# Sixteen experts' gate and up weights in three places instead of two, loaded in fixed order

## The chip, the cores and the metric

The kernel runs on one core of one Trainium2 chip. The metric is the device time of one launch in microseconds, the median of three runs. The core has five engines: TensorE (PE, with its weight loads PEld), VectorE (DVE), ScalarE (ACT), GpSimd (POOL) and SyncE (SP), which here only issues DMA transfers.

## What is computed

The reference is one layer of a hybrid model over 16 meta tokens and 1024 tokens of width 1024: a norm, one projection, three mixers (S5, HGRN2, differential attention), an output projection, and a mixture of experts, then a final norm. The change touches the experts alone:

```python
    group_prob = jax.nn.softmax((t @ w_group).astype(f32) + b_group.astype(f32), axis=-1)
    gp, gi = lax.top_k(group_prob, 1)
    ...
    ev, ei = lax.top_k(in_group, MOE_TOP_K)
    ew = jax.nn.softmax(ev, axis=-1) * gp
    expert_id = gi * MOE_EXPERTS_PER_GROUP + ei
    ...
    for e in range(MOE_EXPERTS):
        he = jax.nn.silu(t @ w_gate[e]) * (t @ w_up[e])
        y = y + gates[:, e:e + 1] * (he @ w_down[e])
```

There are 16 experts in four groups, and each token goes to two experts of one group. An expert has gate and up weights of 1024 x 512 each and down weights of 512 x 1024, all float32: 2 MB each, 6 MB an expert. With the reference's inputs the experts get between 59 and 196 of the 2048 rows. In blocks of 128 rows these are 1, 1, 2, 2, 1, 1, 1, 1, 1, 2, 1, 2, 2, 2, 2, 2 blocks, 24 in all, so experts 4 to 8 have one block each, one after another.

## The kernel before

The first half of the program (projection, mixers, attention, output projection) is the same in both kernels. Then VectorE works out the routing (`dve_route`): the slot of each token-expert pair, the number of blocks of each expert, and tables with one entry for each block. SP waits for `tables_ready`, the other engines read the number of block pairs.

The expert stage runs over the blocks. Every engine has its own instruction stream: blocks 0 and 1 are written out, then a loop over pairs of blocks with two bodies in it (`blocks`), then the last pair. The body of block b holds, on TensorE: the turn of the hidden values of b, gate and up of block b + 1 (8 chunks), the turn of the token rows of b + 2 (L2257), and down of block b (4 chunks). A chunk is 128 rows of weights by 1024 columns. Products are made in three passes from split operands: the higher part of a number (rounded to fp32r) and the lower part (the rest), so each chunk has six products (L2277): four with the higher weights, then two with the lower ones.

The higher part of a chunk is cast by ScalarE (L2323), the lower part is a subtraction of the higher part from the raw weights. Chunks 1, 2 and 3 of every four are subtracted by VectorE (L2375), the fourth by GpSimd (L2220). Both parts go through a ring of four chunks (`RING`); a cast waits until TensorE has used the chunk four before it (`chunk_used`). VectorE also makes the hidden values (L2393), the lower part of the rows (L2381), scales the outputs (L2401) and makes the lower part of the hidden values (L2442). GpSimd also gathers the rows of block b + 2 (L2207) and adds outputs into `h_d` (L2247).

Which place of the raw weights a block reads is a number from a table. Each engine reads it into a register at the head of a body: `buffers` (L2193) reads the table `ebuf` for b and for b + 1, two reads (L2191), between the last operation of the body before and the first cast or subtraction of this one.

SP issues the raw weights. Raw gate and up weights have two places, raw down weights two. For each block, SP reads six table entries (L2174), waits for its place, and issues four gate and up transfers (L2180) and one down transfer (L2185). Where the expert is the same as that of the block before, the transfers are issued with a condition that makes them empty. Each waits until the one before it has landed.

Of the kernel before, what the change touches and what calls it, by code (L numbers as in the profile page):

```python
# [13 lines left out]
F32 = mybir.dt.float32  # L14
F32R = mybir.dt.float32r
BF16 = mybir.dt.bfloat16
I32 = mybir.dt.int32
ACT = mybir.ActivationFunctionType
ALU = mybir.AluOpType
AX = mybir.AxisListType  # L20

P = 128
# [28 lines left out]
C_COS = 976  # L51
# [7 lines left out]
MEM = 48432  # L59
# [4 lines left out]
SPLIT = 5 * D + RING * 2 * D  # L64


def constants():
# [22 lines left out]
    c[:, C_IOTAB:C_IOTAB + NB] = np.arange(NB)  # L90
    inv = (np.float32(1.0) / (np.float32(10000.0) ** (np.arange(0, 64, 2, dtype=np.float32) / np.float32(64)))).astype(np.float32)
# [19 lines left out]
def build(nc, a, out):  # L111
    ctx = ExitStack()
    with ctx:
# [11 lines left out]

        with (nc.sbuf_tensor("below_split", [P, NT * D], F32), nc.sbuf_tensor("split", [P, SPLIT], F32R) as split_tensor,
              nc.sbuf_tensor("below_weights", [P, O_C - NT * D - SPLIT], F32),
              nc.sbuf_tensor("weights", [P, 2 * 3 * D * FF // P], F32) as weights_tensor):
            split, weights = split_tensor, weights_tensor
        with (nc.sbuf_tensor("below_x", [P, O_X], F32), nc.sbuf_tensor("xsplit", [P, 2 * KD * L], F32R) as xsplit_tensor,  # L130
# [10 lines left out]
        MLOE_T = split_at("mix_early_lower", MEM - 512, 512)  # L141
        WOL_T = [split_at("wo_lower%d" % k, O_C + 2 * KD * FF + 1024 * k, 1024) for k in range(KD)]
# [1736 lines left out]
        NEW, OLD, RUN, PRV, BUF, NHALF, NPR = take(NB), take(NB), take(NB), take(NB), take(NB), take(1), take(1)  # L1879
        PCMP = take(NB // 2)  # L1880
# [8 lines left out]
        eblk, ebuf, enew = (sml[:, o:o + NB].bitcast(I32) for o in (506, 570, 398))  # L1889
        efree2 = sml[:, 104:104 + NB].bitcast(I32)  # L1890
        efree, edown, npair = sml[:, 366:366 + NB].bitcast(I32), sml[:, 334:334 + NB].bitcast(I32), sml[:, 504:505].bitcast(I32)
# [36 lines left out]
        def dve_route(dve, link):  # L1928
# [39 lines left out]
            link(ts(BLK[:, 0:2], BLK[:, 0:2], 1.0, None, ALU.max))  # L1968
# [42 lines left out]
            link(nc.vector.tensor_copy(eblk[:, :], EBF))  # L2011

            scan = nc.vector.tensor_tensor_scan
            link(nc.vector.memset(NEW[:, 0:1], 1.0))
            link(tt(NEW[:, 1:NB], EBF[:, 1:NB], EBF[:, 0:NB - 1], ALU.not_equal))
            link(ts(OLD, NEW, -1.0, 1.0, ALU.mult, ALU.add))
            link(tt(PRV, NEW, con[:, C_IOTAB:C_IOTAB + NB], ALU.mult))
            link(scan(RUN, OLD, PRV, 0.0, ALU.mult, ALU.add))
            link(nc.vector.memset(PRV[:, 0:1], 0.0))
            link(tt(PRV[:, 1:NB], NEW[:, 1:NB], RUN[:, 0:NB - 1], ALU.mult))  # L2020
            link(scan(BUF, OLD, PRV, 0.0, ALU.mult, ALU.add))
            link(ts(PRV, BUF, 12.0, 1.0, ALU.mult, ALU.add))
            link(ts(RUN, PRV, 9.0, None, ALU.min))
            link(stt(RUN, PRV, -8.0, RUN, ALU.add, ALU.max))
            link(nc.vector.tensor_copy(efree, RUN))
            link(ts(RUN, RUN, 4.0, None, ALU.add))
            link(nc.vector.tensor_copy(efree2, RUN))
            link(ts(BUF, BUF, 0.0, 12.0, ALU.is_gt, ALU.mult))
            link(tt(PRV, PRV, BUF, ALU.add))
            link(nc.vector.tensor_copy(edown, PRV))  # L2030
            link(tt(OLD, OLD, NEW, ALU.subtract))
            link(scan(BUF, OLD, NEW, 1.0, ALU.mult, ALU.add))
            link(nc.vector.tensor_copy(ebuf, BUF))
            dve_rows_lower(dve, 0, 0)
            link(stt(NEW, EBF, 1.5, NEW, ALU.is_gt, ALU.mult))
            link(nc.vector.tensor_copy(enew, NEW))
            link(ts(NHALF, CB[:, NE - 1:NE], 0.5, None, ALU.mult))
            link(tt(PCMP, NHALF.to_broadcast([P, NB // 2]), con[:, C_IOTAB:C_IOTAB + NB // 2], ALU.is_gt))
            link(red(NPR, PCMP, AX.X, ALU.add))
            link(ts(NPR, NPR, float(-(LEAST // 2)), None, ALU.add))  # L2040
            nc.vector.tensor_copy(npair, NPR).then_inc(tables_ready, 1)

        def dve_slot_hot(dve, link):
# [8 lines left out]
            link(nc.vector.tensor_copy(HOTW[:, :, 0], HOT))  # L2052
            for i in range(3):
# [22 lines left out]
        WGU = weights[:, 0:4 * KD * FF].rearrange("p (k i n) -> p k i n", i=2, n=FF)  # L2076
        WDN = weights[:, 4 * KD * FF:].rearrange("p (k n) -> p k n", n=D)
        oS = NT * D
# [7 lines left out]
        WH, WL = ([take_split(D) for _ in range(RING)] for _ in range(2))  # L2086
# [24 lines left out]
        def raw(kind, k, q):  # L2111
# [3 lines left out]
            if kind == "gu":  # L2115
                return WGU[:, bass.ds(q * KD + k, 1)].rearrange("p a i n -> p (a i n)")
# [38 lines left out]
        def sp_experts(sp):  # L2155
# [10 lines left out]
            sp.dma_start(WDN[:, 0:FF // P], a["w_down"][0].rearrange("(k p) n -> p k n", p=P)).then_inc(first_loaded, 16)  # L2166
            sp.wait_ge(xg_loaded[0], 16)
            sp.dma_start(WDN[:, FF // P:2 * FF // P], a["w_down"][1].rearrange("(k p) n -> p k n", p=P)).then_inc(wdn_loaded, 16)
            sp.wait_ge(first_loaded, 48)
            sp.wait_ge(tables_ready, 1)  # L2170

# [451 lines left out]
```

## Time and profile before

| | |
|---|---|
| median of 3 runs | 1196.14 us (1190.55 to 1201.69) |
| span of the profiled execution | 1192.0 us (its own time is shown as this span) |
| granted TensorE clock, mean | 0.966 |
| PE busy | 1065.8 us (89%) |
| DVE busy | 843.0 us (71%) |
| ACT busy | 638.6 us (54%) |
| POOL busy | 487.2 us (41%) |
| DMA, mean | 164 GB/s |
| L2277, expert products | 1728, 418.1 us busy |
| L2375, lower parts on DVE | 216, 300.9 us busy |
| L2220, lower parts on POOL | 72, 205.0 us busy |

The span is the time from the first to the last instruction of one execution. Busy time is the union of an engine's operations; the ends of matmuls are modelled. The expert stage begins at about 700 us and ends at about 1162 us; before it stand 58% of the span, which the change does not touch apart from the routing tables.

### The profile page before, as it was taken

To read this page: it belongs to the slowest core of one execution; us is meant where nothing else is said; L and a number is where in the kernel's file an instruction comes from. 1 tells how busy PE (TensorE), PEld (TensorE's weight loads), DVE (VectorE), ACT (ScalarE), POOL (GpSimd) and SP (SyncE) were. 2 spreads that over 40 slices of the span, in tenths; PEclk is the share of its full clock that TensorE was granted. 3 is DMA by queue.
4 is the path that set the end of the run, shared out by engine and by line. 5 is a ranking of instruction groups with operands and counts; after the bars stand their busy time and mean duration, and the time that the engine had idled before them with its cause. 6 is when DMAs were issued, how large, how long until landed. Compare 5 with 4: busy or idle time off the path is not lost. (4 is left out here: it accounts for less than half of the span.)

```text
span 1192.0 us, 22049 instructions
## 1 busy us (share of the span) xinstructions
PE 1065.8 (89%) x7126; PEld 888.2 (75%) x7126; DVE 843.0 (71%) x1234; ACT 638.6 (54%) x1008; POOL 487.2 (41%) x303
## 2 busy tenths in 40 slices
PE   4899998999969989999999648999999999999995
PEld 4898998889968646666667536878777887888873
DVE  5797857563357556555554497888887999899987
ACT  5522111166533456444443326778776887888854
POOL 1121211122000226111111114878775887999960
PEclk9999999999988989999999859999999999999988
DMA  7216434332033820011111774788999878877454
GB/s 266 80 48 73 118 95 127 102 114 71 21 72 80 319 71 1 19 54 53 54 66 59 280 267 159 238 257 305 322 379 371 275 266 286 258 266 229 103 160 161
DMA packets 89495, 194.97 MB, mean 164 GB/s; under 512 B 9265, under 2 KB 32049, under 8 KB 88769
## 3 DMA queue, kind: packets, MB, share of 16 engines
q1 hardware_dynamic: 82800, 169.91, 42.0%
q0 software_dynamic: 6624, 24.12, 8.5%
q8 instruction: 45, 0.74, 0.3%
q14 instruction: 26, 0.20, 0.1%
HBM read 220.60 MB, written 31.51 MB: 211 GB/s over the span
## 5 line engine op out<-in xcount | busy, mean ns | idle before, releaser
L2277 PE MATMUL ps<-split 128*128 128x512 f32 x1728 | 418.1, 398 | 15.8 <-DVE split L2375 8.1
L2277 PEld LDWEIGHTS ps<-split 128*128 128x128 f32 x1728 | 322.4, 190 | 93.3 <-DVE split L2375 12.8
L2323 ACT CAST split<-weights 128x1024 fp32r (+1 forms) x288 | 298.2, 1052 | 101.9 <-PE ps L2277 80.4
L2375 DVE TENSOR_TENSOR split<-weights,split 128x1024 fp32r<-128x1024 f32 x216 | 300.9, 1446 | 46.5 <-ACT split L2323 45.0
L480 PE MATMUL ps<-xsplit,wsplit 128*128 128x384 f32 (+2 forms) x1440 | 239.7, 324 | 4.0 <-POOL wsplit L252 4.0
L2220 POOL TENSOR_TENSOR split<-weights,split 128x1024 fp32r<-128x1024 f32 x72 | 205.0, 2847 | 91.4 <-ACT split L2323 90.4
L480 PEld LDWEIGHTS ps<-xsplit,wsplit 128*128 128x128 f32 x1440 | 226.2, 189 | 5.4 <-POOL wsplit L252 4.6
L252 POOL TENSOR_TENSOR wsplit<-mem,wsplit 128x1024 fp32r<-128x1024 f32 x22 | 57.1, 2597 | 247.7 <-ACT wsplit L335 247.7
L1605 DVE TENSOR_REDUCE sml<-ps 128x1 f32<-128x1040 f32 (+7 forms) x64 | 46.6, 769 | 61.6 <-PE ps L1785 61.6
L1722 ACT COPY mem<-ps 128x512 f32<-128x512 f32 (+3 forms) x48 | 21.4, 481 | 109.3 <-PE ps L1804 71.7
L1548 POOL TENSOR_TENSOR sml<-sml 128x4 f32<-128x4 f32 x8 | 8.1, 1015 | 156.2 <-DVE sml L1626 156.2
L335 ACT CAST wsplit<-mem 128x1024 fp32r<-128x1024 f32 x22 | 23.2, 1053 | 85.1 <-DMA mem<-in_w_in 85.1
L2247 POOL DMA_INDIRECT h_d<-par,sml x22 | 53.0, 2408 | 3.4 <-issue 3.0
L1661 ACT ACTIVATE mem<-ps,sml 128x1040 f32<-128x1040 f32 (+7 forms) x64 | 47.1, 736 | 0.0
L1810 PE MATMUL ps<-mem 128*128 128x128 f32 x288 | 39.3, 282 | 7.1 <-ACT mem L1722 7.1
L2207 POOL DMA_INDIRECT con<-xn_d,sml x24 | 37.7, 1571 | 19.3 <-POOL sml L2204 19.3
L1810 PEld LDWEIGHTS ps<-mem 128*128 128x128 f32 x288 | 34.7, 191 | 12.6 <-ACT mem L1722 12.2
L1785 PE MATMUL ps<-mem 64*128 64x400 f32 (+6 forms) x224 | 42.4, 493 | 0.0
L419 ACT COPY mem<-ps 128x384 f32<-128x384 f32 (+2 forms) x48 | 20.3, 451 | 40.9 <-PE ps L480 34.6
L2328 ACT CAST split<-ps 128x512 fp32r<-128x512 f32 x48 | 25.7, 589 | 17.8 <-PE ps L2257 17.8
L1026 POOL TENSOR_TENSOR sml<-sml 128x16 f32<-128x16 f32 x2 | 7.6, 3800 | 66.6 <-DVE sml L1231 66.6
L2401 DVE TENSOR_SCALAR par<-ps,sml 128x512 f32<-128x512 f32 x44 | 30.9, 744 | 5.1 <-DMA h_d<-par,sml 5.1
(434 smaller groups left out, 1631.1 us busy)
## 6 DMA issues: line engine op xcount, KB each, us to landing
weights<-in_w_down SPq DMA_DIRECT2D x26, 2048.0 KB, 15.9
weights<-in_w_gate SPq DMA_DIRECT2D x50, 1024.0 KB
weights<-in_w_up SPq DMA_DIRECT2D x50, 1024.0 KB
mem<-in_w_in SPq DMA_DIRECT2D x22, 512.0 KB, 4.4
mem<-in_x SPq DMA_DIRECT2D x10, 512.0 KB, 3.5
mem<-in_w_out SPq DMA_DIRECT2D x1, 4096.0 KB, 14.8
h_d<-mem SPq DMA_DIRECT2D x8, 512.0 KB, 2.6
xn_d<-mem SPq DMA_DIRECT2D x8, 512.0 KB, 2.6
```

What stands on the lines that cost most here:

```text
L252: nc.gpsimd.tensor_tensor(WLO[i], RAW[i], WHI[i].bitcast(F32), ALU.subtract).then_inc(wlo_ready, 1)
L480: mm = nc.tensor.matmul(ps[:, n % 6, 0:hi - lo], w[slot_of(h)][:, k % 4, P * m:P * m + P], x[:, k, lo:hi], start=(k == 0 and p_ == 0), sto ...
L1605: nc.vector.tensor_reduce(NMX[:, 2 * (n % 2) + c:2 * (n % 2) + c + 1], logits(c)[:, KEY0:KEY0 + keys_of(n)], AX.X, ALU.max, negate=True).t ...
L1661: f(PR_[n % 2][:, c, 0:nk], logits(c)[:, KEY0:KEY0 + nk], ACT.Exp, bias=NMX[:, o:o + 1], accum_out=SUM[:, o:o + 1]).then_inc(exp_done, 1)
L1785: mm = nc.tensor.matmul(logits(c)[:, s:e], AQ[R, h, P * i:P * i + P], AK[R, h, s - lo:e - lo], start=(e != hi), stop=True, skip_group_chec ...
L1810: nc.tensor.matmul(b[:, 0:P], AT[n % 2][:, k], V[:, 1 + k, vc], start=(k == 0), stop=False)
L2207: pool.indirect_dma_start(XG[:, par], None, xn_d, bass.IndirectOffsetOnAxis(ap=ixc[:, par:par + 1], axis=0)).then_inc(xg_loaded[par], 16)
L2220: nc.gpsimd.tensor_tensor(WL[place % RING], raw(kind, k, q), WH[place % RING].bitcast(F32), ALU.subtract).then_inc(wl_pool, 1)
L2247: pool.indirect_dma_start(h1_d, bass.IndirectOffsetOnAxis(ap=sixc[:, 1 - par:2 - par], axis=0), YE, None, compute_op=ALU.add).then_inc(ye_ ...
L2277: mm = nc.tensor.matmul(ps[:, bank + h, :], x, w[place % RING][:, 512 * h:512 * h + 512], start=(k == 0 and p_ == 0), stop=(k == n - 1 and ...
L2323: nc.scalar.copy(WH[place % RING], raw(kind, k, q)).then_inc(wh_ready, 1)
L2375: nc.vector.tensor_tensor(WL[place % RING], raw(kind, k, q), WH[place % RING].bitcast(F32), ALU.subtract).then_inc(wl_dve, 1)
```

## The change

The gate and up weights get a third place, at the start of the memory, where the routing tables are worked out before. Expert e lies in place e mod 3 for gate and up and e mod 2 for down. These two numbers stand in a constant table (`C_GUB`, `C_DNB`) indexed by the expert. The load tables on VectorE go (`ebuf`, `enew`, `efree`, `efree2`, `edown`); one table of the expert of each block (`etab`) and one of when an expert's gate and up are used up (`half_free`) are left. SP's loop over blocks becomes a written-out list over experts: gate and up of e + 1, then down of e. An engine now finds its place by reading the expert of the block, and then the place of that expert. The lower part of the first rows moves from the middle of the tables to the slot weights. An empty expert would get one block; with these inputs there is none.

```diff
-MEM = 48432
+MEM = 48416
...
+UNIT = 128
+GU_AT = (O_C, O_C + 2 * KD * FF, 0)
...
+    c[:, C_GUB:C_GUB + NE] = np.array([GU_AT[e % 3] // UNIT for e in range(NE)], np.int32).view(np.float32)
+    c[:, C_DNB:C_DNB + NE] = np.array([e % 2 for e in range(NE)], np.int32).view(np.float32)
...
-            link(ts(BLK[:, 0:2], BLK[:, 0:2], 1.0, None, ALU.max))
+            link(ts(BLK, BLK, 1.0, None, ALU.max))
...
-            link(nc.vector.tensor_copy(eblk[:, :], EBF))
-
-            scan = nc.vector.tensor_tensor_scan
-            link(nc.vector.memset(NEW[:, 0:1], 1.0))
...
-            nc.vector.tensor_copy(npair, NPR).then_inc(tables_ready, 1)
+            link(nc.vector.tensor_copy(npair, NPR))
+            link(ts(CB, CB, 12.0, float(gu_used(-1) - KD // 2), ALU.mult, ALU.add))
+            nc.vector.tensor_copy(half_free, CB).then_inc(tables_ready, 1)
...
-                for half in range(2):
-                    sp.wait_ge(w_loads[half], 32 * b + 32)
-                    sp.wait_ge(chunk_used, (free, free_second)[half])
...
+            sp.wait_ge(slots_ready, 2)
+            sp_gate_up(sp, 2, None)
+            free = sp_half_free(sp, 0)
+            for e in range(2, NE):
+                if e + 1 < NE:
+                    free_next = sp_half_free(sp, e - 1)
+                    sp_gate_up(sp, e + 1, free)
+                sp_down(sp, e, free)
+                free = free_next
...
+        def expert_of(eng, b):
+            return eng.value_load(etab[0:1, bass.ds(b, 1)], min_val=0, max_val=NE - 1)
 
         def buffers(eng, b, par, last):
 
-            q = buffer_of(eng, b)
-            return q, (buffer_of(eng, b + 1) if has(par, last, 1) else None)
+            e = expert_of(eng, b)
+            q = eng.value_load(dn_at[0:1, bass.ds(e, 1)], min_val=0, max_val=1)
+            if not has(par, last, 1):
+                return q, None, e, None
+            e_next = expert_of(eng, b + 1)
+            return q, eng.value_load(gu_at[0:1, bass.ds(e_next, 1)], min_val=0, max_val=max(GU_AT) // UNIT), e, e_next
...
-                        act.wait_ge(w_loads[k // 4], 32 * b + 96)
+                        act.wait_ge(w_loads[k // 4], 32 * e_next + 32)
```

VectorE, the end of the loop and the head of what follows it, before. `L2381` is the lower part of the rows, `TENSOR_LOAD` a read of a table into a register, the last row the first subtraction of a block:

```order
L2381 TENSOR_TENSOR split<-ps,split 128x512 [waits xh_ready]
L2144 ISA
L2144 COMPARE_AND_BRANCH
L2191 ISA
L2191 TENSOR_LOAD sml
L2191 ISA x3
L2191 TENSOR_LOAD sml
L2191 ISA x2
L2374 ISA
L2375 ISA [waits wh_ready]
L2375 TENSOR_TENSOR split<-weights,split 128x1024
```

The same place in the changed kernel:

```order
L2393 TENSOR_TENSOR split<-ps,split 128x512 [waits xh_ready]
L2131 ISA
L2131 COMPARE_AND_BRANCH
L2199 TENSOR_LOAD sml
L2199 ISA x2
L2204 TENSOR_LOAD con
L2204 ISA x2
L2208 TENSOR_LOAD con
L2208 ISA x2
L2386 ISA
L2387 ISA [waits wh_ready]
L2387 TENSOR_TENSOR weights_lower<-gate_up,weights_higher 128x1024
```

Rows that only repeat are left out: the read of L2199 stands there twice, ahead of L2204 and ahead of L2208, so two reads have become four, each with its own register instructions, and the read of L2204 or L2208 needs the result of the one ahead of it.

SP, one expert of the written-out list in the changed kernel. L2175 reads `half_free`, L2188 is gate and up, L2196 is down:

```order
L2175 TENSOR_LOAD sml
L2175 ISA x2
L2188 DMA gate_up<-in_w_gate 128x4x512 [waits chunk_used,first_half_loaded]
L2188 DMA gate_up<-in_w_up 128x4x512
L2184 REGISTER_ALU [waits chunk_used,second_half_loaded]
L2188 DMA gate_up<-in_w_gate 128x4x512 [waits chunk_used]
L2188 DMA gate_up<-in_w_up 128x4x512
L2194 REGISTER_ALU [waits wdn_loaded]
L2196 DMA weights<-in_w_down 128x4x1024 [waits chunk_used]
```

Before, each block had six such reads (L2174) ahead of the same five transfers; now each expert has one, and there is no loop.

## Rows read from the trace of the kernel before

**Rows 1.** Waits from 690 us on: waiter, releaser, total us, times, longest.
```profile
ACT split L2323 <- DMA weights<-in_w_up: 16.3, 5, 3.8
PE ps L2257 <- DMA con<-xn_d,sml: 7.2, 1, 7.2
```

**Rows 2.** Chain of waits, row turns (L2257): start us, us, what.
```profile
739.64 0.87 PE ps L2257 x8
848.96 0.87 PE ps L2257 x8
927.69 0.87 PE ps L2257 x8
981.30 0.88 PE ps L2257 x8
1002.43 0.87 PE ps L2257 x8
1020.16 0.87 PE ps L2257 x8
1037.89 0.87 PE ps L2257 x8
1055.64 0.87 PE ps L2257 x8
1127.13 0.87 PE ps L2257 x8
```

**Rows 3.** Stretches: us, busy PE, PEld, DVE, ACT, POOL, PEclk, DMA share, GB/s.
```profile
820.00:838.00 18.00, 18.00 (x88) 14.99 (x87) 14.63 (x16) 14.41 (x17) 13.61 (x9) 1.00 0.67 200
848.80:868.60 19.80, 18.48 (x85) 14.46 (x84) 15.85 (x16) 13.86 (x17) 13.07 (x10) 1.00 1.05 376
1020.00:1037.70 17.70, 17.70 (x85) 14.73 (x84) 15.46 (x15) 14.34 (x17) 15.40 (x10) 1.00 0.79 263
```

**Rows 4.** Register reads, L2191, 1037 to 1046: ns min/median/max, first and last start.
```profile
L2191 DVEq TENSOR_LOAD <-sml x2: 307/794/1281, 1040.7 to 1042.4; - x2
L2191 DVEq SEQ_ASSERT  x2: 23/23/23, 1042.2 to 1042.9; - x2
L2191 ACTq SEQ_ASSERT  x2: 18/18/18, 1039.3 to 1039.9; - x2
```

**Rows 5.** Timelines, ordinary turn from 1037.89: start us, us, what [idle before, releaser].
```profile
1043.22 3.50 DVE L2375 TENSOR_TENSOR split<-weights,split 128x1024 fp32r<-128x1024 f32 x3 [1.14 <-ACT split L2323]
1045.80 3.19 POOL L2220 TENSOR_TENSOR split<-weights,split 128x1024 fp32r<-128x1024 f32 x1 [0.47 <-ACT split L2323]
1044.46 1.05 ACT L2323 CAST split<-weights 128x1024 fp32r x1 [0.31 <-PE ps L2277]
1044.45 11.19 PE L2277 MATMUL ps<-split 128*128 128x512 f32 x48
```

**Rows 6.** Timelines, turn from 1055.64, first half of the loop.
```profile
1061.21 3.50 DVE L2375 TENSOR_TENSOR split<-weights,split 128x1024 fp32r<-128x1024 f32 x3 [1.32 <-ACT split L2323]
1063.54 3.44 POOL L2220 TENSOR_TENSOR split<-weights,split 128x1024 fp32r<-128x1024 f32 x1 [0.22 <-ACT split L2323]
1058.56 2.00 ACT L2323 CAST split<-weights 128x1024 fp32r x2 [0.20 <-issue]
```

**Rows 7.** Timelines, turn from 981.30.
```profile
989.29 3.43 DVE L2375 TENSOR_TENSOR split<-weights,split 128x1024 fp32r<-128x1024 f32 x1
989.20 2.44 POOL L2220 TENSOR_TENSOR split<-weights,split 128x1024 fp32r<-128x1024 f32 x1
992.78 6.06 PE L2277 MATMUL ps<-split 128*128 128x512 f32 x24 [1.00 <-DVE split L2375]
1000.31 2.11 PE L2277 MATMUL ps<-split 128*128 128x512 f32 x8 [1.47 <-DVE split L2375]
```

**Rows 8.** Timelines, turn from 1002.43.
```profile
1006.84 3.50 DVE L2375 TENSOR_TENSOR split<-weights,split 128x1024 fp32r<-128x1024 f32 x3 [0.73 <-ACT split L2323]
1010.33 2.40 POOL L2220 TENSOR_TENSOR split<-weights,split 128x1024 fp32r<-128x1024 f32 x1 [1.38 <-ACT split L2323]
```

## What the change does to the time, predicted blind

> **What bounds the kernel now.** I read the waits first, then the chain of waits, then DMA by stretches, then single engines inside one block of the expert stage. All durations are of one profiled execution with a span of 1192.0 us; the median of the runs, 1196.14, is 4.1 above it, and I add that 4.1 at the end.
>
> The waits [rows 1] name what the change aims at: ScalarE stood 16.3 us, in five waits, for gate and up weights. They also show that the first block begins when its gathered rows land (TensorE waits 7.2 us for that DMA), not when a table is ready.
>
> The chain of waits [rows 2] has one row for each turn of token rows (L2257). From one such row to the next I call a turn; there are 21 of them, 739.64 to 1127.13, together 387.5 us. Three kinds are to be seen. Ordinary turns take 17.73 (1020.16 to 1037.89) and 17.75. The four turns 848.96 to 927.69 take 78.7, or 19.7 each: those are the experts with one block each. The turn from 981.30 takes 21.13, with an expert of two blocks, and it is the one that decides my forecast.
>
> The stretches [rows 3] explain the slow four: DMA runs at 376 GB/s with its share full, against 263 in an ordinary turn. 19.8 us at 376 GB/s are 7.4 MB; in 17.7 us this would take 420 GB/s, more than any stretch shows. Before them, 820 to 838, it runs at 200. So loads that start earlier can remove this loss.
>
> **Inside a turn** TensorE is fed through a ring of four chunks: ScalarE casts, VectorE subtracts for three of four, GpSimd for the fourth. Take t = 0 at the turn's L2257 row. In the turn 1037.89 [rows 5], TensorE starts gate and up at 6.56 (1044.45), and a chunk takes 1.37 (48 products in 11.19, with 0.2 of the last one's tail). The lower parts come in its last two products of six, so it needs subtraction 1, 2, 3 by 7.5, 8.8, 10.2. VectorE starts the first at 5.33 and does three in 3.50, so the third begins at 5.33 + 2.28 = 7.6. GpSimd asks for its own subtraction, the fourth, at 7.91, after ScalarE's cast that starts at 6.57. It is 0.3 us after VectorE's third has begun.
>
> The turn from 981.30 shows what happens in the other order [rows 7]. GpSimd asked at 989.20 (7.90), VectorE's third subtraction came at 989.29 (7.99) and took 3.43 us instead of 1.2: it stood still for nearly the whole of GpSimd's 2.44. TensorE waited 1.0 and later 1.47, when the same thing happened at the second group of chunks. The page SBUF — State Buffer of the Trainium skill (SBUF: two separate sides) says that a VectorE operation with two SBUF inputs and a GpSimd operation share a port pair that the first holds to its end; the trace agrees, 3.43 against 1.2. So a turn costs 17.73 when VectorE comes first and 21.13 when GpSimd does: **3.4 us for being 0.09 us late**.
>
> How near is the edge elsewhere? In the turn 1055.64, the first half of the loop [rows 6], the third begins at 5.57 + 2.28 = 7.85 and GpSimd asks at 7.90: 0.05 us of margin. In the turn right after a collision [rows 8] VectorE is ahead: first subtraction at 4.41, third at 6.69, GpSimd at 7.90, margin 1.2.
>
> **The change, part by part.**
>
> *Third place and fixed order of loads.* It removes SP's six table reads for each block, and it lets gate and up of expert e + 1 go out ahead of down of e. With the reference's inputs every expert has rows, so both kernels load sixteen experts and compute the same 24 blocks: no byte and no product is added. The four turns can fall from 78.7 to 4 x 17.73 = 70.9: gain **7.8 us**, at most 16.3 by the waits. I take 7.8; the rest of the waits was hidden behind the ring.
>
> *Shorter table chain on VectorE before the first block.* About 25 small operations go. The first block starts at the landing of the rows [rows 1], so I count 0; expert 2's load now waits for the second slot table instead, and has a whole block until its use: 0.
>
> *Reads from tables in each block.* VectorE, ScalarE and GpSimd read two numbers into registers for each block now, and four after it. This is the price. On VectorE they stand between the last row subtraction and the first weight subtraction, and VectorE is idle during them. The first read takes 1.28 because it waits for the engine to drain; the second takes 0.31, and the checks behind the two follow each other at 0.7 [rows 4]. Two more reads are **1.4 us** more before the first subtraction of each block. Bounds: 0 if they overlapped with something, 2 x 1.28 = 2.6 if each one waited like the first. I take 1.4, the spacing of neighbours; with nothing in flight the second is like the third. On ScalarE the spacing is 0.6, so 1.2 us; its casts then run back to back and are in step again by the fourth, except in the first half of the loop, where its first cast already starts late (1058.56, t = 2.92). There the fourth cast, and GpSimd's request, slip by some 0.45. On GpSimd the reads run beside its own subtraction: 0.
>
> The page DMA: Bandwidth & Descriptors (Latency and other measured facts) puts a register read at about 600 ns. By it the price would be 1.2 us, and the third subtraction after a collision would begin at 7.89, level with GpSimd's 7.90. The sum would then be that of my second case below. The trace's 0.7 decides.
>
> *What 1.4 us do.* Ordinary turn: the third begins at 9.0, the second at 7.9, GpSimd asks at 7.9 to 8.0: a collision at the third or even at the second. Loop-start turn: 9.3 against 8.35: a collision. Ordinary turn after a collision: 8.1 against 7.9, a collision by 0.2. Loop-start turn after a collision: 8.1 + 0.24 (the difference of the two kinds now) = 8.3 against 8.35, undecided.
>
> Price. After a collision: VectorE's second ends its hold at 8.1, GpSimd holds 2.3, the third is ready at 11.6 against a need of 10.2. That is what the turn from 981.30 had (its third ended at 992.72, t = 11.4), so 3.4 and 21.1 in all. Coming from an undisturbed turn the third is ready at 5.33 + 1.4 + 3.50 + 2.3 = 12.5, 1.1 later: 22.2. A turn that escapes still gets its fourth chunk later, since GpSimd waits for VectorE's third: 0.3 to 1.5, so 18.7.
>
> Sum over pairs of turns. Loop-start: half 21.3, half 18.7, mean 20.0. The other half of the loop: 21.1 or 22.2, mean 21.65. Mean of both **20.8**, against 18.45 now; 21 x 20.8 = 437. Outside the 21 turns 1192.0 - 387.5 = 804.5 stay. Span 1241.5, with the 4.1 **1245 us**. The 7.8 us gained are inside this: a turn of 20.8 us moves 7.4 MB at 356 GB/s, below the 376 seen, so the loads stop being a bound in any case, and the third place has nothing left to save.
>
> **The rivals.**
>
> A. *The collision alternates*: a turn after a collision always escapes (reads a little cheaper, or ScalarE later than I think). Mean (17.9 + 22.2)/2 = 20.05 down to (17.75 + 21.1)/2 = 19.4; times 21 is 407 to 421, and the time 1216 to 1230. For it: a margin of 0.2 us decides. Against: the spacing of 0.7. Chance 0.20, taken as 1205 to 1230.
>
> B. *Faster: the reads are hidden*, through VectorE's sequencer running ahead of the engine as ScalarE's does. It decides at a delay under the margins, 0.05 and 0.3 us. Then 1192.0 - 7.8 + 4.1 = 1188, and with all 21 turns at 17.75 it is 804.5 + 372.8 + 4.1 = 1181. For it: ScalarE's two reads cost nothing visible. Against: VectorE's first read of 1.28 us, and an idle gap of 1.14 before each first subtraction [rows 5]. Chance 0.20; 0.12 of it under -1%, 0.08 within 1%.
>
> C. *The change does not do what it says*: down still has two places and one queue carries all loads, so the waits stay, and nothing else moves: 1196. For it: at 376 GB/s the four turns are bound by bandwidth itself. Against: 200 GB/s just before them. Chance 0.04.
>
> D. *Collisions at both groups in every turn*, above 1268: 0.04.
>
> My own case, collisions in most turns, 1230 to 1268, keeps 0.52.
>
> **The numbers.** Forecast 1245. The range 1190 to 1268 takes my case, A, C and the upper part of B: about 0.79; my case's own range is 1230 to 1268. No change is 1184 to 1208, about what runs between 1190.55 and 1201.69 can tell. Faster 0.12, same 0.12, slower 0.76.
>
> **What would show it.** Right: ScalarE's waits for weights gone; DMA under 376 GB/s in 849 to 928; four reads on VectorE for each block and the first subtraction at t = 5.8 to 6.8; GpSimd's fourth subtraction starting before VectorE's third, subtractions of 3.4 us in most turns, TensorE idle with VectorE as releaser, turns of about 21. Wrong: turns of 17.7 with four reads in them, or reads that end while row subtractions still run; then B holds, and my step from reads to 1.4 us fails. If turns are long and no subtraction takes 3.4, the price has another cause.

## The result and the profile after

| | before | after |
|---|---|---|
| median | 1194.34 us (1190.55 to 1201.69, 4 runs) | 1230.64 us (1228.19 to 1240.27, 4 runs) |
| ratio to before | 1 | 1.0308, 95% interval 1.0272 to 1.0344 |
| span of the profiled execution | 1192.0 us | 1230.8 us (its own time is 1232.65) |
| granted TensorE clock, mean | 0.966 | 0.959 |
| 21 turns from the same block on | 387.5 us | 420.4 us |
| the rest of the span | 804.5 us | 810.4 us |

The change made the kernel slower by 3.1%. A turn, as in the prediction, is the time from one row of the token rows' turn to the next; in the changed kernel this line is L2269.

The waits of the changed kernel from 690 us on (waiter, releaser, total us, times, longest):

```profile
DVE weights_lower L2387 <- ACT weights_higher L2335: 60.1, 41, 2.9
PE ps L2289 <- DVE weights_lower L2387: 32.4, 27, 1.5
ACT weights_higher L2335 <- issue: 21.2, 11, 2.2
PE ps L2269 <- DMA con<-xn_d,sml: 7.2, 1, 7.2
ACT weights_higher L2335 <- DMA gate_up<-in_w_up: 2.6, 2, 1.7
```

The change did what it was made for: ScalarE's waits for gate and up weights fell from 16.3 us [rows 1] to 2.6. In their place TensorE waits for VectorE's lower parts, 32.4 us in 27 waits, with 1.5 us the longest. The first block still begins when its rows land, after the same 7.2 us.

The chain of waits of the changed kernel, row turns (start us, us, what), where [rows 2] has those of before:

```profile
864.02 0.87 PE ps L2269 x8
885.27 0.87 PE ps L2269 x8
906.82 0.87 PE ps L2269 x8
924.93 0.87 PE ps L2269 x8
946.58 0.87 PE ps L2269 x8
964.66 0.87 PE ps L2269 x8
986.38 0.87 PE ps L2269 x8
1004.50 0.88 PE ps L2269 x8
1026.16 0.87 PE ps L2269 x8
```

The differences are 21.25, 21.55, 18.11, 21.65, 18.08, 21.72, 18.12 and 21.66: from the third row on, long and short turns take each other's place. Over all 21 turns, 10 are long (over 21 us, mean 21.75) and 11 short (mean 18.45). In each of the 10 long ones, and in no short one, VectorE's first three subtractions took 5.70 us or more instead of 3.50.

The reads into registers, VectorE's queue, 906 to 925 us, the counterpart of [rows 4] (line, queue, operation, times: ns min/median/max, first and last start):

```profile
L2199 DVEq TENSOR_LOAD <-sml x2: 307/325/343, 909.6 to 911.1; - x2
L2199 DVEq SEQ_ASSERT  x2: 23/23/23, 910.2 to 911.6; - x2
L2204 DVEq SEQ_ASSERT  x1: 23/23/23, 910.9 to 910.9; - x1
L2208 DVEq SEQ_ASSERT  x1: 23/23/23, 912.4 to 912.4; - x1
```

Four reads, each closed by a check: 910.2, 910.9, 911.6, 912.4, so 0.7 us from one to the next.

A short turn, from 906.82: timelines of the first group of chunks (start us, us, what [idle before, releaser]), to be held against [rows 5] and [rows 6]:

```profile
912.62 3.50 DVE L2387 TENSOR_TENSOR weights_lower<-gate_up,weights_higher 128x1024 fp32r<-128x1024 f32 x3 [2.12 <-ACT weights_higher L2335]
914.89 3.50 POOL L2232 TENSOR_TENSOR weights_lower<-gate_up,weights_higher 128x1024 fp32r<-128x1024 f32 x1 [1.70 <-ACT weights_higher L2335]
910.73 3.89 ACT L2335 CAST weights_higher<-gate_up 128x1024 fp32r x4 [1.18 <-PE ps L2289]
```

VectorE's row holds three subtractions. The third begins at 912.62 + 2.28 = 914.90, which is t = 8.08; GpSimd's row begins at 914.89, t = 8.07. They come together, VectorE is served first (its three take the usual 3.50) and GpSimd's takes 3.50 instead of 2.4 us. The releaser named for VectorE's idle 2.12 us is ScalarE, but ScalarE's first cast had ended at 911.8; the idle time is the reads.

The next turn, from 924.93, is a long one, the counterpart of [rows 7]:

```profile
931.19 5.70 DVE L2387 TENSOR_TENSOR weights_lower<-gate_up,weights_higher 128x1024 fp32r<-128x1024 f32 x3 [1.89 <-ACT weights_higher L2335]
933.29 2.51 POOL L2232 TENSOR_TENSOR weights_lower<-gate_up,weights_higher 128x1024 fp32r<-128x1024 f32 x1 [1.47 <-ACT weights_higher L2335]
936.94 0.74 PE L2289 MATMUL ps<-weights_lower,split 128*128 128x512 f32 x2 [1.48 <-DVE weights_lower L2387]
944.47 0.73 PE L2289 MATMUL ps<-weights_lower,split 128*128 128x512 f32 x2 [1.47 <-DVE weights_lower L2387]
```

The third subtraction wants to begin at 931.19 + 2.28 = 933.47; GpSimd began at 933.29, 0.18 us before. The three subtractions take 5.70 us instead of 3.50, and TensorE waits 1.48 us, then 1.47 at the second group.

DMA in the stretch of the experts with one block each (us, busy PE, PEld, DVE, ACT, POOL, PEclk, DMA share, GB/s), beside [rows 3]:

```profile
868.00:928.00 60.00, 54.44 (x250) 42.77 (x249) 52.64 (x44) 42.44 (x48) 40.14 (x28) 1.00 1.03 362
```

TensorE is busy for 54.44 of these 60 us at full clock, although ScalarE hardly waits for a weight.

### The profile page after: what moved, and what is told of

It reads as the page before. It is cut to its first block and busy times, and to the rows that moved or that the text cites. A ratio compares the mean times of both kernels' runs of the same rounds, so it can differ in the third digit from the quotient of the medians.

```text
span 1230.8 us, 21639 instructions
## 1 busy us (share of the span) xinstructions
PE 1084.5 (88%) x7126; PEld 893.5 (73%) x7126; DVE 867.0 (70%) x1212; ACT 634.6 (52%) x1008; POOL 466.4 (38%) x303
## 5 line engine op out<-in xcount | busy, mean ns | idle before, releaser
L2289 PE MATMUL ps<-weights_higher,split 128*128 128x512 f32 x1152 | 318.5, 399 | 5.2 <-DVE split L2454 2.9
L2387 DVE TENSOR_TENSOR weights_lower<-gate_up,weights_higher 128x1024 fp32r<-128x1024 f32 x144 | 217.8, 1564 | 54.8 <-ACT weights_higher L2335 54.8
L2289 PEld LDWEIGHTS ps<-weights_higher,split 128*128 128x128 f32 x1152 | 216.1, 191 | 50.6 <-issue 5.0
L2335 ACT CAST weights_higher<-gate_up 128x1024 fp32r (+1 forms) x192 | 193.7, 1049 | 87.0 <-PE ps L2289 64.6
L2289 PE MATMUL ps<-weights_lower,split 128*128 128x512 f32 x576 | 187.7, 407 | 33.9 <-DVE weights_lower L2387 32.4
L2232 POOL TENSOR_TENSOR weights_lower<-gate_up,weights_higher 128x1024 fp32r<-128x1024 f32 x48 | 129.7, 2701 | 108.3 <-ACT weights_higher L2335 108.3
L2289 PEld LDWEIGHTS ps<-weights_lower,split 128*128 128x128 f32 x576 | 104.2, 190 | 78.9 <-DVE weights_lower L2387 49.5
L2335 ACT CAST weights_higher<-weights 128x1024 fp32r x96 | 100.9, 1051 | 54.3 <-PE ps L2289 50.8
L2387 DVE TENSOR_TENSOR weights_lower<-weights,weights_higher 128x1024 fp32r<-128x1024 f32 x72 | 109.6, 1571 | 5.3 <-ACT weights_higher L2335 5.3
L2232 POOL TENSOR_TENSOR weights_lower<-weights,weights_higher 128x1024 fp32r<-128x1024 f32 x24 | 68.8, 2866 | 26.0 <-ACT weights_higher L2335 25.6
## 6 DMA issues: line engine op xcount, KB each, us to landing
mem<-in_w_out SPq DMA_DIRECT2D x1, 4096.0 KB, 14.5
```

What stands on the lines that cost most here:

```text
L2232: nc.gpsimd.tensor_tensor(WL[place % RING], raw(kind, k, q), WH[place % RING].bitcast(F32), ALU.subtract).then_inc(wl_pool, 1)
L2289: mm = nc.tensor.matmul(ps[:, bank + h, :], x, w[place % RING][:, 512 * h:512 * h + 512], start=(k == 0 and p_ == 0), stop=(k == n - 1 and ...
L2335: nc.scalar.copy(WH[place % RING], raw(kind, k, q)).then_inc(wh_ready, 1)
L2387: nc.vector.tensor_tensor(WL[place % RING], raw(kind, k, q), WH[place % RING].bitcast(F32), ALU.subtract).then_inc(wl_dve, 1)
```

## The experiments

Kernels that were measured together shared a chip and the runs of the kernel before. Its medians beside the experiments lay between 1194.47 and 1201.26 us, so each kernel is judged by its ratio. All gains are under 2%; one is called a gain where its whole interval lies below 1. The last column is 21 turns from the same block on, read from the profiled execution.

| kernel | us, median | ratio to before (95%) | 21 turns, us |
|---|---|---|---|
| before | 1194.34 | 1 | 387.5 |
| after | 1230.64 | 1.0308 (1.0272 to 1.0344) | 420.4 |
| e1 before, VectorE +2 reads | 1243.51 | 1.0358 (1.0322 to 1.0395) | 430.8 |
| e2 before, ScalarE +2 reads | 1200.45 | 0.9988 (0.9942 to 1.0034) | 390.0 |
| e3 after, GpSimd waits in all groups | 1243.91 | 1.0361 (1.0323 to 1.0399) | 434.5 |
| e4 after, VectorE 2 reads, tables ahead | 1198.00 | 0.9982 (0.9944 to 1.0019) | 384.5 |
| e5 before, VectorE +1 read | 1221.31 | 1.0186 (1.0144 to 1.0229) | 412.4 |
| e6 after, short GpSimd subtraction | 1181.16 | 0.9866 (0.9828 to 0.9904) | 373.0 |
| e7 three places, one packed read | 1180.51 | 0.9845 (0.9803 to 0.9886) | 374.2 |
| e8 two places, one packed read | 1185.78 | 0.9904 (0.9867 to 0.9940) | 384.3 |
| e9 before, +2 reads on three engines | 1234.91 | 1.0329 (1.0290 to 1.0369) | 425.8 |
| e10 after, four reads on VectorE only | 1245.15 | 1.0421 (1.0378 to 1.0464) | 431.0 |
| e11 after, GpSimd waits in first group | 1215.09 | 1.0148 (1.0095 to 1.0202) | 407.3 |
| e12 three places, VectorE two packed reads | 1183.81 | 0.9893 (0.9849 to 0.9936) | 378.6 |

**e1 and e2: which engine's reads cost.** The kernel before, with two reads more at the head of a body, on VectorE (e1) or on ScalarE (e2):

```diff
                 q, q_next = buffers(dve, b, par, last)
+                for _ in range(2):
+                    buffer_of(dve, b)
```

> The kernel before, with two more register reads on VectorE at the head of each block and nothing else; their values are not used. If VectorE's later first subtraction and the collision with GpSimd cost the time: first subtraction 1.4 us later, turns that alternate between 17.9-19.3 and 21-22.3 us, subtractions of 3.4 us, and about the time of the changed kernel or more, 1225 to 1245 us, since the four turns bound by weights stay near 19.7. If the time comes from the new order or place of the loads: 1190 to 1200 us, as before.

> The kernel before, with two more register reads on ScalarE alone, values not used. If only VectorE's lateness counts: no loss, 1188 to 1198 us, and perhaps a little gain, since GpSimd's request comes later in the turns that begin the loop and the two collisions may go. If reads cost on any engine: 1.2 us in each of 22 blocks, 1215 to 1225 us.

Two reads on VectorE, with loads and places untouched, cost 3.6% and TensorE's waits for VectorE's lower parts rose from 8.1 to 48.2 us. Two on ScalarE cost nothing that the whole time can show. So the loss is the reads on VectorE.

The turns of e2 say that its even result is a balance. The turn of 21.1 us is gone. It and four others that begin the loop now take 18.9 to 19.3 us; those four took 17.7 to 18.4 before. ScalarE's casts in the turn from 1051.7:

```profile
1057.07 3.90 ACT L2323 CAST split<-weights 128x1024 fp32r x4 [2.63 <-PE ps L2277]
```

The first cast starts at t = 5.4, where [rows 6] has 2.92, after 2.63 us of idle time with the reads in it. VectorE then starts late because it waits for casts, and GpSimd asks 0.7 us behind VectorE's third subtraction in all five turns, so nothing collides.

The timelines of e1, turn from 992.28, show how little decides:

```profile
997.87 3.50 DVE L2375 TENSOR_TENSOR split<-weights,split 128x1024 fp32r<-128x1024 f32 x3 [1.92 <-ACT split L2323]
1000.19 3.44 POOL L2220 TENSOR_TENSOR split<-weights,split 128x1024 fp32r<-128x1024 f32 x1 [2.01 <-ACT split L2323]
```

The third subtraction began at 1000.15, GpSimd asked at 1000.19: 0.04 us later, and the turn took 17.90.

**e3: force the order.** The changed kernel, and GpSimd's subtraction waits for VectorE's third of its group:

```diff
             def lower(b, place, kind, k, q):
+                if b is not None:
+                    pool.wait_ge(wl_dve, counts(b, place)[1])
                 pool.wait_ge(wh_ready, counts(b, place)[0] + 1)
```

> The changed kernel with one more wait on GpSimd: its subtraction of each fourth chunk waits until VectorE has done the third of the same four. If the collision is the cost: no subtraction of 3.4 us on VectorE as the third of a group, turns of 18.2 to 19.3 us like those of the changed kernel that escaped, and 21 x 1.3 to 1.8 us less, 1195 to 1205 us. If the cost is VectorE's 1.4 us less time in each block, with the collision only a symptom: 1225 to 1240 us, as the changed kernel or worse.

This missed. No third subtraction was held any more, yet all turns took 19.6 to 21.2. The waits of e3 say why:

```profile
PE ps L2291 <- POOL weights_lower L2234: 41.6, 43, 1.3
PE ps L2291 <- DVE weights_lower L2389: 7.9, 12, 1.9
```

TensorE now waits for GpSimd's chunk. The two engines do their subtractions one after the other in either order, and moving the order moves the wait to the other's chunk. GpSimd's subtraction also begins later here than it would by itself: 1.6 us behind the start of VectorE's third, which takes 1.2.

**e4: two reads with three places.** Tables with one entry for each block, worked out on VectorE ahead of the first block; VectorE reads two numbers, ScalarE and GpSimd still four:

```diff
+            for at, tab, first in ((C_GUD, gtab, GU_AT[0] // UNIT), (C_DND, dtab, 0)):
+                link(tt(EPL, ECMP, con[:, at:at + NE].unsqueeze(1).to_broadcast([P, NB, NE]), ALU.mult))
+                link(red(FPL, EPL, AX.X, ALU.add))
...
-                q, q_next, _, _ = buffers(dve, b, par, last)
+                q = dn_place(dve, b)
+                q_next = gu_place(dve, b + 1) if has(par, last, 1) else None
```

> The changed kernel with tables of places by block, made on VectorE before the first block (eight more small operations there, about 3.6 us), so that VectorE reads two numbers for each block as the kernel before; ScalarE and GpSimd still read four. Loads in three places in fixed order stay. If the two extra reads on VectorE are the whole loss: turns of 17.7 to 17.9 us with the odd collision, the four turns of single-block experts too, and 1180 to 1190 us, below the kernel before. If the loads cause the loss: 1225 to 1235 us.

The loss of the change is gone, the gain I expected is not there: 1198.0, level with before. The four turns of experts with one block did fall to 70.9 us from 78.7, and VectorE is never held in the first group of any turn. But six other turns take 18.4 to 18.9 us with the sign of e2: GpSimd asks 0.7 us behind VectorE's third, and in the one from 1020.5 ScalarE is idle for 2.58 us before its first cast. So ScalarE's four reads are part of the price. The table operations stand from 709.83 to 714.03 us, 4.2 us of VectorE's time; e12 below takes both leftovers away.

**e5: one read more.** The edit of e1 with one read:

> The kernel before, and VectorE reads its place table once more at the head of each block (three reads instead of two); nothing else changes. Threshold theory: the first subtraction comes 0.7 us later, which is more than both margins (0.3 and 0.05 us), so the loss is most of that of two more reads: collisions of 3.4 us in about every second turn, the turns between them at 17.7 to 18, time 1220 to 1240. Rival, lateness costs in proportion: every turn longer by about the same 0.7 to 1.0 us, no long subtractions, 1215 to 1222. Rival, one read is hidden: 1190 to 1205.

1221.3: about half of e1's loss for half of its reads, so the total alone would fit a cost in proportion. The turns don't: those of 17.7 and of 21.5 to 23.1 alternate for the most part, with one of 19.6 and one of 18.1, and none lies at the 18.5 that a proportional cost would give. The two longest, 22.8 and 23.1, lie among the experts with one block and had no collision in the first group; the other seven long ones had.

**e6: take GpSimd's hold away, leave VectorE late.**

```diff
+                n = slice(0, 64 if b is not None else D)
-                nc.gpsimd.tensor_tensor(WL[place % RING], raw(kind, k, q), ...
+                nc.gpsimd.tensor_tensor(WL[place % RING][:, n], raw(kind, k, q)[:, n], ...
```

> The changed kernel with its four reads, but from block 0's body on GpSimd subtracts only 64 of the 1024 columns of the fourth chunk; the other columns keep old values, so this part of the computation is left out. If the loss comes from GpSimd's subtraction holding VectorE's (and the other way round), it must go although VectorE still starts 1.4 us late: no subtraction of 3.4 us, turns of 17.7 to 18.5, 1185 to 1205. If it comes from VectorE being late in itself (TensorE waits for the first lower part, or ScalarE's casts are late), turns stay at 19.5 or more and the time over 1215.

1181.2, below the 1185 that I had expected at the least, and this run carries most of the cause. Timelines of e6, turn from 850.45:

```profile
856.20 3.50 DVE L2388 TENSOR_TENSOR weights_lower<-gate_up,weights_higher 128x1024 fp32r<-128x1024 f32 x3 [2.08 <-ACT weights_higher L2336]
858.47 1.40 POOL L2233 TENSOR_TENSOR weights_lower<-gate_up,weights_higher 128x64 fp32r<-128x64 f32 x1 [1.74 <-ACT weights_higher L2336]
```

VectorE starts at t = 5.75, as late as in the changed kernel, after the same 2.1 us of reads, and the turn takes 17.72. Being 1.4 us late costs VectorE nothing in itself. What costs is GpSimd's 2.4 us inside VectorE's row. (e6 also makes GpSimd's own chunk ready sooner. That this is not what helps is in the waits of the changed kernel: TensorE waited 32.4 us for VectorE's chunks and 0.7 for GpSimd's.) SBUF — State Buffer of the Trainium skill (SBUF: two separate sides) says that the one that comes first holds the shared ports for its whole instruction and the other stands still; the trace agrees in both directions: VectorE's 1.2 us became 3.43, and GpSimd's 64 columns took 1.40 us while VectorE was ahead of it and 0.32 in another turn.

**e7 and e8: one packed number.** Both places and both experts of a block stand in one table entry. e7 has three places and builds the table on VectorE where it waits in the first block; e8 is the kernel before with its two places packed.

```diff
+            v = eng.value_load(code[0:1, bass.ds(b, 1)], min_val=0, max_val=1 << 20)
+
+            def field(shift, mask, hi):
+                return eng.snap(((v >> shift) & mask if shift else v & mask).with_bounds(min_val=0, max_val=hi))
+
+            q, e = field(0, 1, 1), field(12, 15, NE - 1)
```

> The changed kernel (three places, fixed order of loads), but both places and both experts of a block stand in one packed number of a table with one entry for each block, worked out on VectorE while it waits in the first block; each engine reads one number for each block and takes it apart with register operations. One read on VectorE instead of four, the first subtraction 0.7 us earlier than in the kernel before. Theory of margins: nearly all turns 17.7, the four turns of experts with one block too unless bandwidth holds them, 1172 to 1190. Rival, the register operations cost as much as the reads: 1200 to 1240. Rival, something else than the reads was lost by three places: over 1200 with no long third subtractions.

> The kernel before (two places, loads as before) with the two places of a block packed in one number, one read instead of two on VectorE, ScalarE and GpSimd. If third place and fixed order are worth the 7.8 us of the four slow turns, this kernel stays 5 to 10 us above the packed one with three places: 1180 to 1195. If they are worth nothing, the two are equal within 3 us. The collision turn of the kernel before (21.1 us) should be gone in both.

e7 beats both kernels: 0.9845 of before. 20 of its 21 turns take 17.7 us. Its timelines, turn from 869.41, in the stretch that was bound by loads before:

```profile
873.67 3.50 DVE L2393 TENSOR_TENSOR weights_lower<-gate_up,weights_higher 128x1024 fp32r<-128x1024 f32 x3 [0.59 <-ACT weights_higher L2340]
877.41 2.43 POOL L2237 TENSOR_TENSOR weights_lower<-gate_up,weights_higher 128x1024 fp32r<-128x1024 f32 x1 [1.63 <-ACT weights_higher L2340]
```

The third subtraction begins at 875.95, 1.46 us ahead of GpSimd. What the third place is worth shows in the same stretch of both kernels, first e7, then e8:

```profile
849.00:869.00 20.00, 20.00 (x95) 16.61 (x94) 17.48 (x17) 16.29 (x18) 16.84 (x11) 1.00 1.04 377
```

```profile
849.00:869.00 20.00, 18.02 (x81) 14.32 (x80) 14.31 (x15) 13.25 (x16) 10.83 (x9) 0.96 1.04 372
```

Both are at the DMA rate of 372 to 377 GB/s, but e7 has room for the gate and up weights of one expert more, and TensorE never stops. In e8 the four turns from 851.95 to 930.50 take 78.6 us instead of 4 x 17.73 = 70.9, and ScalarE waits for weights in them; in e7 it has no such wait after 690 us. The wait of e8 from 849 to 932 us:

```profile
ACT split L2328 <- DMA weights<-in_w_up: 12.9, 4, 4.6
```

Over 21 turns e7 is 10.1 us shorter than e8; the medians differ by 5.3, and the two intervals meet, so the runs bound the third place's worth less well than the turns do. For e8 against the kernel before it is the other way round: its median is 11.6 us lower, its 21 turns only 3.2 us shorter (384.3 against 387.5). Where the rest of that gain lies the traces don't show.

**e9 and e10: why the changed kernel lost less than e1.** e9 is e1's edit in `buffers`, so on all three engines. e10 is e7 with the four dependent reads put back on VectorE alone.

```diff
-                q, q_next, _, _ = buffers(dve, b, par, last)
+                q, q_next, _, _ = buffers_by_expert(dve, b, par, last)
```

> The kernel before (two places) with two more reads at the head of each block on VectorE, ScalarE and GpSimd alike, so the number of reads of the changed kernel without its third place. The changed kernel lies 13 us under the kernel with two more reads on VectorE alone (1230.6 against 1243.5). If the whole 13 is the third place and the order of loads, this one comes to 1240 to 1248. If the whole 13 is the slip of ScalarE's fourth cast (GpSimd then asks later and collides less), it comes to 1228 to 1234. I expect a part of each: 1234 to 1242, turns in 848 to 928 about 1 us longer than in the changed kernel.

> The changed kernel where VectorE reads four numbers at the head of each block as before, but ScalarE and GpSimd read one packed number. Slip theory: ScalarE's casts are early again, GpSimd asks at 7.9 to 8.2 in every turn, turns after a collision escape by less and collide more often: 1228 to 1242, not faster than the changed kernel, with fewer reads in it. Rival, each engine's reads cost time of their own: 1215 to 1226. Under no theory does it come near 1200, since VectorE's reads stay.

e10 has six reads fewer for each block than the changed kernel (three fewer on ScalarE, three on GpSimd) and is 14.5 us slower, 3 above the range that I had expected. 14 of its turns are over 21 us, against 10. Its timelines in the turn from 870.40:

```profile
876.21 5.71 DVE L2404 TENSOR_TENSOR weights_lower<-gate_up,weights_higher 128x1024 fp32r<-128x1024 f32 x3 [2.14 <-ACT weights_higher L2351]
878.38 2.45 POOL L2248 TENSOR_TENSOR weights_lower<-gate_up,weights_higher 128x1024 fp32r<-128x1024 f32 x1 [1.99 <-ACT weights_higher L2351]
```

GpSimd begins at t = 7.98 and the third subtraction wants to at 8.09. VectorE stands as in the changed kernel's turn from 906.82 (8.08), but GpSimd comes 0.09 us earlier, and the turn takes 21.22 instead of 18.11. So the reads on ScalarE, which delay its fourth cast and with it GpSimd, saved the changed kernel some of its collisions. The turns of e9 say the same with two places: 425.8 us for 21 turns against e1's 430.8, and 11 long ones against 14; the ratios of these two overlap and don't part them.

**e11: order the first group only.** The edit of e3 with `place == RING - 1` added.

> The changed kernel, and GpSimd's fourth subtraction of the first group of chunks waits for VectorE's third of that group; the second and the third group stay as they are. The kernel that waited in all three groups took 1243.9, 13 more than the changed kernel, without any collision in the first group. If what it lost came from the waits in the second group and in down, this one is better than the changed kernel: 1205 to 1225, no subtraction of 3.4 us in the first group. If the order itself costs as much as a collision (GpSimd's 2.4 us then begin after VectorE's third has ended, and TensorE waits for the fourth chunk), it stays at 1225 to 1245.

1215.1: half of the changed kernel's loss comes back, and e3's miss is placed: the 2.1% by which it is slower than e11 (27 us in the 21 turns) were the waits in the second group and in down. The waits of e11:

```profile
PE ps L2291 <- POOL weights_lower L2234: 11.6, 21, 0.7
PE ps L2291 <- DVE weights_lower L2389: 10.9, 13, 1.7
```

**e12: two reads, three places, cheap tables.** e7 with VectorE's read made twice.

> The kernel with packed numbers and three places, but VectorE reads its number twice at the head of a block: two reads as in the kernel before, with the third place, and the table hidden in the first block. It stands beside the kernel with per-block tables that took 1198.0 (two reads on VectorE, four on ScalarE and GpSimd, tables worked out before the first block). If that one lost its gain to ScalarE's four reads and to the tables, this one shows the gain that three places have with two reads: 1180 to 1190, a few turns with a collision left since the margins are 0.05 to 0.3 us again. If two reads on VectorE are themselves too many with three places, it is at 1194 to 1200.

1183.8, ratio 0.9893. With the reads of before on VectorE, three places gain 1.1% (ScalarE and GpSimd have one packed read here, where they had two). Its 21 turns are 8.9 us shorter than those of before. The spans of e4 and e12 differ by 17.0 us (1199.0 and 1182.0). Of these, 7.2 had come up in the first half of the program, which the two share; 2.0 lie between there and the first of the 21 turns, where e4 has its tables, 5.9 in the 21 turns and 2.0 behind them. So the tables' 4.2 us cost no more than 2.0, and the larger part, 5.9, goes with the reads of ScalarE and GpSimd, four in e4 and one in e12.

## Why the prediction was right, and by how much it was off

The forecast was 1245 us and slower; 1230.6 was measured, slower. The direction and the mechanism were right. That the time falls into my own case's range is luck: it is 0.6 us above its lower end of 1230, and there were collisions in 10 turns of 21, not in most. By its steps:

- **The third place and the order of loads, 7.8 us gained.** Right in mechanism and size. The four turns took 70.9 us in e4, e7 and e12, against 78.7 before and 78.6 in e8; over 21 turns e12 is 8.9 us shorter than before and e7 10.1 shorter than e8. That nothing of it is left once turns take 20 us is less sure. The changed kernel moved 362 GB/s from 868 to 928, below the 377 of e7, and e10 (three places) and e1 (two) took the same, 431.0 and 430.8 us for 21 turns. But the changed kernel's turns are 5.4 us shorter than those of e9, which has its reads and two places; their ratios, 1.0308 and 1.0329, don't part them.
- **Two more reads on VectorE, 1.4 us.** Right: 0.7 us from check to check in the changed kernel. After a collision the first subtraction moved from t = 4.41 [rows 8] to 5.80. The page DMA: Bandwidth & Descriptors of the Trainium skill (Latency and other measured facts) gives about 600 ns as the floor of a `tensor_load`. Here the `TENSOR_LOAD` rows themselves took 0.31 to 0.34 us, and from check to check, which is what the engine loses, it was 0.7.
- **The reads on ScalarE, 1.2 us that are made good by the fourth cast.** Too small for the turns that begin the loop. I had GpSimd's request slip by 0.45 there; in e2 the first cast moved from t = 2.92 to 5.4 and the turns became about 1 us longer without any collision. It is also the likely reason why the changed kernel's short turns took 18.45 on average: in e10, without those reads, they took 18.04.
- **The collision, 3.4 us for being late by a tenth.** Right, and the experiments make it the cause: e1 brings the loss without the change, e6 takes it away with the reads left in. Long turns took 21.2 to 22.3 us, where I had 21.1 to 22.2.
- **The ordinary turn after a collision.** This step failed, on which of the two engines comes first. I put the third subtraction at 8.1 against GpSimd's 7.9, "a collision by 0.2", and so counted three quarters of the turns, about 16 of 21, as long. There were 10. VectorE was where I had it (8.08); GpSimd was not at 7.9 but at 8.07. I had seen that ScalarE's reads let its fourth cast slip, but allowed for it only in the first half of the loop ("its casts then run back to back and are in step again by the fourth"). In the turn from 906.82 its four casts do run back to back, 910.73 to 914.62, but end at t = 7.80; the fourth cast of [rows 5] ended at 7.62. e10, without those reads, has GpSimd at 7.98 and 14 long turns. The changed kernel had five ordinary turns right after a collision, and all five escaped: in two GpSimd asked level with VectorE's third, within 0.02 us, in three 0.7 us behind it.
- **The size of it.** 21 turns took 420.4 us, not 437: 16.6 us less. Outside the turns the span was 5.9 us longer than I had left it; 4.8 of that had come up before any changed instruction (rows below). 1241.5 - 16.6 + 5.9 = 1230.8, the span. The 4.1 us that I added for the median were not there.

My rival A, the alternation, with a chance of 0.20, described the pattern better than my own case did: its mean turn was 19.4 to 20.05, the measured one is 20.02. It named the reason too ("ScalarE later than I think"). I had it right that a margin of 0.2 us decides, and chose the wrong side of it. Rival B, hidden reads, is out (e1). Rival C, that the change does nothing, is out (e12).

Single turns outside this pattern, such as the one of 19.57 us in e7, collide at the second group of chunks, for another reason. Timelines of e7, turn from 778.9:

```profile
788.68 1.41 DVE L2419 TENSOR_SCALAR par<-ps,sml 128x512 f32<-128x512 f32 x2 [1.98 <-DMA h_d<-par,sml]
790.61 5.69 DVE L2393 TENSOR_TENSOR weights_lower<-gate_up,weights_higher 128x1024 fp32r<-128x1024 f32 x3
```

VectorE waits 1.98 us for the transfer that adds the last block's outputs before it can write new ones, and then its third subtraction of the second group comes behind GpSimd's. Every such wait of 1.9 us or more in the 21 turns of the kernel before, e4, e7, e8 and e12 (eight of them) made a turn of 19.6 to 20.8 us; with waits up to 1.53 us a turn of these kernels, the four experts with one block aside, took at most 18.1. What stays open is why that transfer is late in those blocks, and the part of e8's gain that its turns don't show.

## What to carry to other kernels

Before adding an instruction to the head of a loop body, find the two engines that exclude each other there and measure the gap between their requests: with 0.05 to 0.3 us of margin, two cheap reads on VectorE became 42 us (e1). Where such a margin exists, widening it is worth something by itself: with one packed read on VectorE (e7) instead of two (e12) the 21 turns are 4.4 us shorter. And take the cost away while leaving the delay in, as e6 did: with the table of waits beside it, one run tells lateness from exclusion.

## What the runs showed of the hardware

- Of VectorE's and GpSimd's subtractions, the one that asks first is served first, down to hundredths. Take the start of GpSimd's fourth subtraction against the start of VectorE's first plus 2.28 us, in the first group of all 21 turns of the kernel before, the changed one, e1, e2, e4, e5, e7, e8, e9, e10 and e12, 231 turns. In all 57 turns in which GpSimd was ahead by 0.03 us or more, VectorE's three took 5.7 us; in all 174 others, with GpSimd at most 0.02 us ahead, they took 3.5 to 3.9.
- Fewer instructions, here on ScalarE and GpSimd, can make a kernel slower: e10 against the changed kernel, 1245.15 against 1230.64 us.
- Taking a register apart costs less than one more read: 0.19 against 0.42 us. e7, VectorE's queue, 870 to 888 us, one read with all four numbers in it:

```profile
L2205 DVEq TENSOR_LOAD <-sml x1: 416/416/416, 872.6 to 872.6; - x1
L2205 DVEq FUSED_REGOPS  x1: 190/190/190, 873.0 to 873.0; - x1
```

- Transfers made empty by a condition show in one count and not in another. The kernel with two places has ten of them a program (blocks 0 and 1, and the eight second blocks of experts), and the profile's line on HBM reads, first of e8, then of the changed kernel, differs by 62.9 MB, ten times the 6.29 MB of an expert, while DMA packets and bytes are the same within 0.03 MB. The kernel before has the 220.60 MB of e8. That the empty transfers are what is counted is worked out from this sum, no run takes them away alone:

```profile
HBM read 220.60 MB, written 31.51 MB: 212 GB/s over the span
```

```profile
HBM read 157.70 MB, written 31.51 MB: 154 GB/s over the span
```

- The first half of the program, the same in all kernels, takes more or less time from one execution to the next. The same reduction near its end, in the timelines of e2 and of the changed kernel:

```profile
653.69 0.69 DVE L1625 TENSOR_REDUCE sml<-mem 128x4 f32<-128x512 f32 x1 [2.92 <-ACT mem L1735]
```

```profile
661.02 0.69 DVE L1634 TENSOR_REDUCE sml<-mem 128x4 f32<-128x512 f32 x1 [2.92 <-ACT mem L1744]
```

In the kernel before it began at 656.18, in e4 at 663.40. The undisturbed turns of e7 lie within 17.70 and 17.75 us, so turns are the better measure of the stage.
